# Row-grouped indexer scores, up-projected rotated halves, paired key norms and an exp/ln gate in a two-layer hybrid decoder

## What is computed

```python
for l in range(2):                        # x: (1, 512, 1024) float32
    x = x + token_mix(rms_norm(x), ...)   # three head groups, one input and one output projection
    x = x + square(relu(rms_norm(x) @ w_up)) @ w_down

# token_mix; proj = h @ w_in, split in columns
o_gla = rms_norm(gla(g_q, g_k, g_v, log_a)) * silu(g_gate)         # 4 heads x 128, chunks of 64
rel   = relu(einsum('bqhd,bsd->bqhs', iq, ik))                     # indexer: 8 heads of 32, one key
score = einsum('bqhs,bqh->bqs', rel, iw)                           # summed over heads, weighted
o_dsa = softmax attention over the 128 best causal keys of score   # 4 heads of 64
q_m   = heads(rms_norm(m_cq) @ mla_w_uq)                           # 192 -> 4 x 96 (64 + 32 rotary)
kv_m  = heads(rms_norm(m_ckv) @ mla_w_ukv)                         # 128 -> 4 x (64 key + 64 value)
q_m   = rms_norm(q_m); k_m = rms_norm(concat(k_nope, k_rope))      # over 96, per head
q_m, k_m: last 32 of 96 rotated: x1*cos - x2*sin, x2*cos + x1*sin  # k_rope shared by the heads
o_mla = causal softmax attention                                   # 4 heads, values of 64
out   = concat(o_gla, o_dsa, o_mla) @ w_out
```

## Time and profile before

| | |
|---|---|
| runs | 1363.98, 1358.61, 1358.93 us; median 1358.93 |
| the profiled execution | 1362.79 us, span 1361.1 us, mean granted clock 0.991 |
| TensorE matmul busy | 1305.0 us, 96% of the span, 5952 matmul records |
| VectorE, ScalarE, POOL busy | 812.4, 548.3, 252.3 us |
| DMA | 110.35 MB, 81 GB/s on average |

### The profile page before, as it was taken

One profiled execution on the slowest core, in us unless ns is written; L12 is line 12 of the kernel. 1 busy time (PEld: TensorE's weight loads), 2 busy tenths in 40 slices (PEclk: granted clock), 3 DMA queues, 4 the chain that ended last, 5 costly groups with the idle time before them and its releaser, 6 DMA issues.

```text
span 1361.1 us, 19335 instructions
## 1 busy us (share of the span) xinstructions
PE 1305.0 (96%) x5952; PEld 997.3 (73%) x5952; DVE 812.4 (60%) x1252; ACT 548.3 (40%) x875; POOL 252.3 (19%) x159
## 2 busy tenths in 40 slices
PE   4999999889999999999999999998999999999997
PEld 3755577568888888888885656874788888888886
DVE  4568887744454454544755888967345544445448
ACT  4465344744322313323434644357343232242334
POOL 5022231002011020110530322400020201102016
PEclk9999999989999999999999999999999999999999
DMA  5211121002332222322321111200132322232233
GB/s 199 94 32 63 47 78 47 1 16 95 114 104 97 93 92 95 105 92 92 107 81 62 63 47 62 94 1 1 47 117 98 102 92 93 92 103 97 92 102 129
DMA packets 31025, 110.35 MB, mean 81 GB/s; under 512 B 3568, under 2 KB 3568, under 8 KB 30832
## 3 DMA queue, kind: packets, MB, share of 16 engines
q1 hardware_dynamic: 29088, 103.82, 22.9%
q0 software_dynamic: 576, 3.63, 0.7%
q10 hardware_dynamic: 1296, 2.12, 0.5%
HBM read 107.46 MB, written 2.10 MB: 80 GB/s over the span
## 4 chain that ended last, share of the span: by engine, by line
PE 91%; DVE 3%; issue 2%; ACT 2%; POOL 1%; DMA 1%; DVEq 0%; ACTq 0%; SPq 0%; POOLq 0%
PE bank L816 17%; PE bank L815 17%; PE bank L817 17%; PE bank L477 6%; PE bank L479 6%; PE bank L478 6%; PE bank L511 2%; PE bank L603 2%; PE bank L499 2%; PE bank L500 2%; PE bank L498 2%; PE bank L704 1%; PE bank L731 1%; PE bank L716 1%; PE bank L688 1%
## 5 line engine op out<-in xcount | busy, mean ns | idle before, releaser
L870 ACT ACTIVATE wh<-raw 128x1024 fp32r<-128x1024 f32 x194 | 204.8, 1056 | 396.4 <-PE bank L817 239.0
L1132 DVE TENSOR_TENSOR wl<-raw,wh 128x1024 fp32r<-128x1024 f32 x158 | 247.0, 1563 | 96.1 <-ACT wh L870 88.5
L815 PE MATMUL bank<-hh,wl 128*128 128x512 f32 x512 | 200.0, 391 | 0.0
L815 PE MATMUL bank<-xmh,wl 128*128 128x512 f32 x512 | 199.3, 389 | 0.0
L817 PE MATMUL bank<-xml,wh 128*128 128x512 f32 x512 | 199.2, 389 | 0.0
L817 PE MATMUL bank<-hl,wh 128*128 128x512 f32 x512 | 199.2, 389 | 0.0
L816 PE MATMUL bank<-xmh,wh 128*128 128x512 f32 x512 | 199.2, 389 | 0.0
L816 PE MATMUL bank<-hh,wh 128*128 128x512 f32 x512 | 199.2, 389 | 0.0
L445 POOL TENSOR_TENSOR x<-x,rsb 128x512 f32<-128x512 f32 x64 | 86.7, 1355 | 578.2 <-DVE rsb L1496 578.2
L477 PE MATMUL bank<-xgh,wl 128*128 128x512 f32 x368 | 151.1, 411 | 24.0 <-DVE xgl L1141 18.4
L1485 DVE TENSOR_TENSOR sqb<-tf 128x512 f32<-128x512 f32 x64 | 44.3, 692 | 181.4 <-ACT hh L1103 181.4
(11 more groups left out here) (186 smaller groups left out, 1862.6 us busy)
## 6 DMA issues: line engine op xcount, KB each, us to landing
raw<-in_stream SPq DMA_DIRECT2D x194, 512.0 KB, 3.3
x<-in_x ACTq DMA_DIRECT2D x8, 256.0 KB, 12.8
out_y<-x SPq DMA_DIRECT2D x8, 256.0 KB, 4.1
par<-in_params POOLq DMA_DIRECT2D x2, 788.0 KB, 4.7
con<-in_consts POOLq DMA_DIRECT2D x1, 1200.5 KB, 9.7
par<-in_params POOLq DMA_DIRECT2D x1, 768.0 KB, 11.6
par<-in_params ACTq DMA_DIRECT2D x1, 20.0 KB, 2.5
```

The lines of the kernel that those rows point to most:

```text
L815: pe.matmul(B.t[s][:], wl[:, s, n_block(k)], src_h[:, k], start=(k == 0), stop=False)
L870: act.activation(wh[:, s], raw[:, s], ACT.Copy).then_inc(hi_ready.sem, 1)
L1132: vec.tensor_tensor(wl[:, s], raw[:, s], wh[:, s], ALU.subtract).then_inc(lo_ready.sem, 1)
```

## The change

Five edits are in the diff:
- **Relevance.** The index key is copied to the four groups of 32 partitions of one tile `ikr`. A head's matmul now contracts over its own 32 partitions of `iqT` and `ikr` only. `relevance(g)` waits for four vacant banks (2 to 5) and issues four heads. The six groups stand before, in the middle of, or behind units 7, 8 and 9. ScalarE's relus (`relevant(g)`) go to a new tile `rel` of three buffers, and both they and VectorE's additions (`weighted(g)`) are spread over slots 6, 7 and 8. The memset of `ikp` goes.
- **Rotated halves.** The up-projection's weights get 32 more columns per head, a copy of the rotary columns with swapped halves, so `mq` has 128 rows; `mrot` and its matmul go. The sign stands in the sine table, which lies on partitions 96 to 127 beside the cosine. The bank is now freed by VectorE's `mla_turn`.
- **Key norms by pairs.** The up-projection weights are laid out with keys and values apart, two heads' keys to a matmul; one statistic per pair, with the block matrix `blk`. ScalarE's `key_factor` writes the first head's factor a second time for the rotary rows.
- **Gate.** sigmoid(x) as exp(min(x, 0) - ln(1 + exp(-|x|))).
- **Order.** `mla_v` moves up by two units, the selection steps begin in slot 9 and end in slot 21. ScalarE waits for `gg_ready` before its first exponentials of attention.

```diff
+W_UK = W_UQ + 2 * H * P
+W_UV = W_UK + H * NOPE
...
-    + [(f"rel{i}", 2 + i % 2) for i in range(3 * IDX_H)]
+    + [(f"rel{i}", 2 + i % 4) for i in range(3 * IDX_H)]
...
-                pool.memset(ikp[:], 0.0).then_inc(zeroed.sem, 1)
...
-                for i, (qb, h) in enumerate(REL):
-                    pe.wait_ge(*B.vacant(l, f"rel{i}"))
-                    n = (qb + 1) * P
-                    pe.matmul(B[f"rel{i}"][:, 0:n], iqT[:, h // 4, qb * P:(qb + 1) * P], ikp[:, h % 4, 0:n],
-                              start=True, stop=True).then_inc(*B.on_fill(f"rel{i}"))
-                unit(7)
+                def relevance(g):
+                    for i in range(4 * g, 4 * g + 4):
+                        pe.wait_ge(*B.vacant(l, f"rel{i}"))
+                    for i in range(4 * g, 4 * g + 4):
+                        qb, h = REL[i]
+                        n = (qb + 1) * P
+                        r = slice(32 * (h % 4), 32 * (h % 4) + 32)
+                        pe.matmul(B[f"rel{i}"][:, 0:n], iqT[r, h // 4, qb * P:(qb + 1) * P], ikr[r, 0:n],
+                                  start=True, stop=True).then_inc(*B.on_fill(f"rel{i}"))
+                def midway(g):
+                    return lambda k: relevance(g) if k == KB // 2 else None
+                relevance(0)
+                unit(7, before=midway(1))
...
-                unit(8)
+                relevance(2)
+                unit(8, before=midway(3))
...
-                unit(9)
+                relevance(4)
+                unit(9, before=midway(5))
...
-                def mla_q_rest(h):
+                def mla_q_stat(h):
                     stat(l, f"mqst{h}", ones[0:QK, 0:QK], sq_of(f"mqst{h}")[0:QK], QK)
-                    pe.wait_ge(*qg_ready.at(l, h))
-                    pe.wait_ge(*B.vacant(l, f"mrot{h}"))
-                    pe.matmul(B[f"mrot{h}"][64:QK], con[64:QK, C_ROT:C_ROT + ROPE], tf[64:QK, h % 2],
-                              start=True, stop=True).then_inc(*B.on_fill(f"mrot{h}"))
...
+                def mla_k(pr):
+                    c = W_UK + pr * 2 * NOPE
+                    pe.matmul(B[name][:], par[:, c:c + 2 * NOPE], ckvn[:], start=True, stop=True)\
...
+                def mla_k_stat(pr):
+                    pe.matmul(B[name][:], blk, sq_of(name), start=True, stop=False)
+                    pe.matmul(B[name][:], ones[64:QK, :], cqn[64:QK, 1], start=False, stop=True)\
...
+                def relevant(g):
+                    for i in range(4 * g, 4 * g + 4):
+                        act.wait_ge(*B.filled(l, f"rel{i}"))
+                        if i >= 3:
+                            act.wait_ge(*rel_used.at(l, i - 3))
+                        act.activation(rel[:, i % 3, 0:n], B[f"rel{i}"][:, 0:n], ACT.Relu)\
...
+                def mla_turn(h):
+                    vec.wait_ge(*q_copied.at(l, h))
+                    vec.tensor_tensor(tf[64:QK, h % 2], tf[64:QK, h % 2], cos, ALU.mult)
+                    vec.scalar_tensor_tensor(qT[64:QK, h], B[f"mq{h}"][QK:P, :], gain(G_MQ, QK, P), sin,
+                                             ALU.mult, ALU.mult).then_inc(*B.on_read(f"mq{h}"))
...
+                        link(act.activation(gate_of(h), gg[:, h], ACT.Abs))
+                        link(act.activation(gate_of(h), gate_of(h), ACT.Exp, scale=-1.0))
+                        act.activation(gate_of(h), gate_of(h), ACT.Ln, bias=ones[:, 0:1]).then_inc(gexp_ready.sem, 1)
...
-                per_slot = {7: 5, 8: 4, 9: 4, 10: 3, 11: 3, 12: 4, 13: 4, 14: 4, 15: 4, 16: 2, 17: 2, 18: 2,
-                            19: 2, 20: 5}
+                per_slot = {9: 4, 10: 4, 11: 4, 12: 4, 13: 4, 14: 4, 15: 4, 16: 4, 17: 3, 18: 3,
+                            19: 3, 20: 4, 21: 3}
```

More of the change, by code:

```diff
@@ L194 @@
 NORMS = (["cqst", "ckvst", "dqst0", "mqst0", "dqst1", "mqst1", "dkst0", "mqst2", "dkst1", "mqst3"]
-         + [f"mkst{h}" for h in range(H)] + [f"gst{h}" for h in range(GLA_H)]
+         + ["mkst0", "mkst1"] + [f"gst{h}" for h in range(GLA_H)]
          + [f"aost{b}" for b in range(4)])
@@ L246, in build_trunk @@
         iqT, a0 = place("iqT", [P, 2, T])
-        ikp, _ = place("ikp", [P, 4, T])
+        ikr, _ = place("ikr", [P, T])
+        rel, _ = place("rel", [P, 3, T])
         st, _ = place("st", [P, NCHUNK, 2, GLA_DV], at=a0)
@@ L560, in mla_k_stat @@
                     pe.wait_ge(*B.vacant(l, name))
-                    pe.matmul(B[name][0:QK], ones[0:NOPE, 0:QK], sq_of(name)[0:NOPE], start=True, stop=False)
-                    pe.matmul(B[name][0:QK], ones[64:QK, 0:QK], cqn[64:QK, 1], start=False, stop=True)\
+                    pe.matmul(B[name][:], blk, sq_of(name), start=True, stop=False)
+                    pe.matmul(B[name][:], ones[64:QK, :], cqn[64:QK, 1], start=False, stop=True)\
                         .then_inc(*B.on_fill(name))
@@ L637, in _ @@
                 alone(pe)
-                pe.matmul(B["krot"][64:QK], con[64:QK, C_ROT:C_ROT + ROPE], kT[64:QK, 2],
-                          start=True, stop=True).then_inc(*B.on_fill("krot"))
+                pe.matmul(B["krot"][QK:P], con[64:QK, C_ROT:C_ROT + ROPE], kT[64:QK, 2],
+                          start=True, stop=True, tile_position=(64, QK)).then_inc(*B.on_fill("krot"))
                 mla_k(0)
@@ L944, in tasks @@
                         act.activation(glrs[:], B["glr"][0:RANK, :], ACT.Copy).then_inc(*B.on_read("glr"))
-                        for i, (qb, h) in enumerate(REL):
-                            n = (qb + 1) * P
-                            act.wait_ge(*B.filled(l, f"rel{i}"))
-                            if i >= 2:
-                                act.wait_ge(*rel_used.at(l, i - 2))
-                            act.activation(sqb[:, i % 2, 0:n], B[f"rel{i}"][:, 0:n], ACT.Relu)\
-                                .then_inc(*B.on_read(f"rel{i}"))
+                        relevant(0)
+                        relevant(1)
                     if u == 7:
@@ L996, in tasks @@
                         factor("mqst3", QK, QK)
-                        square("mkst0", B["mk0"][0:NOPE, :], slice(0, NOPE), wait=B.filled(l, "mk0"))
-                    if 14 <= u <= 17:
-                        if u < 17:
-                            h = u - 13
-                            square(f"mkst{h}", B[f"mk{h}"][0:NOPE, :], slice(0, NOPE), wait=B.filled(l, f"mk{h}"))
-                        factor(f"mkst{u - 14}", QK, QK)
-                    if u in (17, 18):
-                        i = u - 17
+                        square("mkst0", B["mk0"][:], wait=B.filled(l, "mk0"))
+                    if u == 14:
+                        square("mkst1", B["mk1"][:], wait=B.filled(l, "mk1"))
+                    if u in (14, 15):
+                        key_factor(u - 14)
+                    if u in (15, 16):
+                        i = u - 15
                         act.wait_ge(*B.filled(l, f"mv{i}"))
@@ new lines, in log_gate, with weighted @@
+                def log_gate(h):
+                    vec.wait_ge(*gexp_ready.at(l, h))
+                    vec.scalar_tensor_tensor(gate_of(h), gg[:, h], 0.0, gate_of(h), ALU.min, ALU.subtract)\
+                        .then_inc(gmin_ready.sem, 1)
+                def silu(h):
+                    vec.wait_ge(*sig_ready.at(l, h))
+                    vec.tensor_tensor(gg[:, h], gg[:, h], gate_of(h), ALU.mult).then_inc(gg_ready.sem, 1)
+                def weighted(g):
+                    for i in range(4 * g, 4 * g + 4):
+                        qb, h = REL[i]
+                        n = (qb + 1) * P
+                        dst = scores_of(qb)
+                        vec.wait_ge(*B.freed(l, f"rel{i}"))
+                        after(vec.scalar_tensor_tensor(dst, rel[:, i % 3, 0:n], iws[:, qb - 1, h:h + 1],
+                                                       causal(qb) if h == 0 else dst, ALU.mult, ALU.add),
+                              rel_used.sem, rel_used.at(l, i)[1])
@@ L1270, in tasks @@
                         evacuate("cq", cqn[:, 0])
-                        for i, (qb, h) in enumerate(REL):
-                            n = (qb + 1) * P
-                            dst = scores_of(qb)
-                            vec.wait_ge(*B.freed(l, f"rel{i}"))
-                            after(vec.scalar_tensor_tensor(dst, sqb[:, i % 2, 0:n], iws[:, qb - 1, h:h + 1],
-                                                           causal(qb) if h == 0 else dst, ALU.mult, ALU.add),
-                                  rel_used.sem, rel_used.at(l, i)[1])
+                        weighted(0)
+                        weighted(1)
                     if u == 7:
@@ L1614, in constant_block @@
         c[64 + half * r:64 + half * (r + 1), C_COS:C_COS + T] = np.cos(ang)
[L1615 removed]
+        c[QK + half * r:QK + half * (r + 1), C_COS:C_COS + T] = np.sin(ang) * (2 * r - 1)
     return c
```

169 lines of the change are left out of this document (93 added, 76 removed), and 15 rows, old and new, of the table USES.

## The result

| | before | after |
|---|---|---|
| median of 7 runs each, measured side by side | 1359.22 us | 1343.55 us |
| lowest to highest | 1358.61 to 1364.52 | 1340.75 to 1352.68 |
| the profiled execution, its span, its mean clock | 1362.79, 1361.1, 0.991 | 1343.55, 1341.9, 0.983 |

The ratio is 0.9874, with an interval from 0.9853 to 0.9896: faster by 1.3%, 15.7 us between the medians, 19.2 between the two profiled spans. The prediction was 34.6 us and a range from 1308 to 1341. The sign was right, the size less than half, and the time outside the range.

A forecast was written before the change was run, and what follows sets the result against it. It took TensorE as the bound, busy 1305.0 of 1361.1 us, so only its work or waits count. 2 x (9.3 behind unit 9 + 8.0 in relevance) = 34.6 us off the median 1358.9 gave 1324.3 us, range 1308 to 1341.

The forecast's parts named there:

- items 1 and 2: Behind unit 9: dropping four rotation matmuls gains 3.9 us per layer, key norms by pairs 6.1.
- I take 0.7: At the second value bank: TensorE waits 0.7 us per layer for VectorE to free the second key pair's bank.
- the blocking of VectorE by POOL: Rival in units 7 to 9: relevance additions held by POOL's low parts, up to 11 us per layer slower, 1381; chance 0.03.
- zero by itself: The gate by exp and ln, behind unit 9: no gain of its own, as TensorE waits for none of it.
- Item 4, row groups: Relevance, units 7 to 9: four heads side by side take 1.06 us with 512 columns; six groups 5.1 us.
- Item 4, waits: Relevance, units 7 to 9: four TensorE waits of 0.9, 1.35, 3.2 and 1.65 us, 7.1 per layer.
- Gain 8.0: Relevance to unit 9's end: 33.6 us where it was 41.6, so 8.0 us per layer gained.
- TensorE's clock falls: Rival: the 3.2 us wait lowers the clock, some 1.7 us each, up to four times, 1331; within the forecast's 0.59.
- VectorE becomes the bound: Rival behind unit 9: VectorE keeps its idle times, items 1 to 3 give nothing, 1342.9 us; chance 0.12.
- Items 1 to 3: Behind unit 9: rotated halves, key norms by pairs and the gate together give 9.3 us per layer.
- One by one: Rival in relevance: matmuls of a group run in a row, gaining 2.9 us per layer there, 1334.5; chance 0.10.
- Attention itself changed in length: Sign of a wrong prediction: attention, taken as unchanged and given no gain, differs in length.

The follow-up runs named there:

- Experiment 3: The changed kernel with POOL's low part of each weight unit cut into four instructions of 128x256: 1332.15 us, ratio 0.9780.
- experiment 2: The changed kernel with six of the 48 selection steps moved from slots 12 to 15 to later slots: 1330.25 us, ratio 0.9771.
- Experiment 4: The changed kernel with the old gate (exponential, plus one, VectorE's reciprocal and product): 1355.4 us, ratio 0.9954.
- Experiment 6: The changed kernel with every relevance matmul on partitions 0 to 31, in the same order and places: 1363.94 us, ratio 1.0004.
- experiment 5: The changed kernel with all six relevance groups behind unit 6, all relus and additions in slot 6: 1360.48 us, ratio 0.9995.
- experiment 7: The changed kernel with ScalarE's two squares of the query latent moved between the first two groups of relus: 1344.62 us, ratio 0.9884.
- experiment 9: The changed kernel with later selection steps, earlier squares of the query latent and four relu buffers for three: 1320.32 us, ratio 0.9689.
- experiment 10: The changed kernel with later selection steps and four relu buffers, the squares left in place: 1319.34 us, ratio 0.9685.
- experiment 11: The changed kernel with later selection steps, earlier squares, four relu buffers and POOL's low parts in four pieces: 1316.06 us, ratio 0.9655.
- experiment 12: The kernel of experiment 9 with the second value bank computed three times over: 1317.93 us, ratio 0.9683.

## Why the prediction was wrong, point by point

**The account.** Forecast 34.6 us, measured 19.2 between the profiles, so 15.4 are missing. The two places of half clock cost 11.9, attention lost 3.4 less than before, so 8.5 are half clock and 6.9 the rest; 5.1 of these lie in the two stretches. In layer 1, with what the half clock cost taken out (3.4 and 2.8 us): the first is 32.5 (forecast 33.6), the second 107.2 (forecast 103.5). The second can be checked by its parts: 112.8 - 11.3 for items 1 and 2 + 5.6 of wait = 107.1.

- **Items 1 and 2, rotations and key norms: right.** Forecast 10.0 us per layer; with TensorE busy throughout, the stretch is 101.5 where it was 112.8, so 11.3. Of the 1.3 more, 0.8 are rotations: what stands between two units fell from 4.86 to 3.72 us in three places and from 3.78 to 2.48 in the fourth, 1.14 and 1.30 for a rotation priced at 0.97. The rest lies with the keys.
- **Item 3, "I take 0.7": this step failed.** It measured 5.6 us in each layer, and 2.8 and 2.3 us of half clock behind it. The layout had VectorE behind in slots 12 to 15, at the right place, with the right bank as the victim. It priced each instruction by its free duration. The prediction had the blocking of VectorE by POOL among its rivals, but asked it of the relevance additions alone ("one low part held up one addition"). It did not go through the slots of its own layout for instructions that read two tiles of SBUF and come beside a low part. There were eight per layer, where there had been two. The gate's new instruction, "about 0.7", measured 2.2 on average. Experiment 3 shows the cause; in experiment 2 the load fitted, once most of the holds had gone. The prediction had named the sign of this step failing: TensorE waiting for `kT` by more than 3 us per layer.
- **Item 3, "zero by itself": wrong in this kernel.** Experiment 4 puts the new gate at 11 to 12 us: with the old one, VectorE comes late to attention (5.1 us of waits on `gvt`). At 90% full, as the prediction had the stretch, the cover had no room for four reciprocals of 3.34.
- **Item 4, row groups: right.** 1.07 and 0.86 us for groups with 512 and 384 columns, forecast 1.06 and 0.85 from the pair of the earlier trace rows. By the Trainium skill's 3.07 ("TensorE: Matmul & The Clock Gate", section "Measured speedup vs the span model") it would be 1.12, an estimate. The "0.5 us a layer less good" that the prediction made of it is a slip: with its own prices the six groups come to 2 x (1.12 + 0.83 + 0.56) = 5.0 us, as its 5.1. The two changes of tiling mode don't show in a group; the unit's next matmul starts a step late (58.97 - 58.63 = 0.34 where a step is 0.23), so 0.11 per group in place of 0.32.
- **Item 4, waits: near, 4.7 us per layer for 7.1.** Measured 0.52 (0.9 forecast), 1.43 (1.35), 2.73 (3.2) and none (1.65). Missing was what the third does to the clock: 3.4 us. "Gain 8.0" measured 5.8.
- **The rival "TensorE's clock falls"** named the wait of 3.2 us, and 1.7 us each, up to four times. There were four stretches, of 3.4 us of lost clock each: two behind that wait, two at the value bank, partly within its wait. Its price came from one stretch of 4 us with clock 0.64, though the same trace has one of 6.8 us at half clock, from 950 to 957 (0.53, 0.50 and 0.50 in three stretches of 2 us, 0.77 in the next). At 11.9 us it would have been 1336 against the median, still inside the range: the half clock alone did not take the time out of it, the wait on `kT` came on top.
- **"VectorE becomes the bound", 1342.9,** has the measured time to within 1 us, which is luck, as the sum behind it is another. Items 1 to 3 did not give nothing: they gave 2.8 of 9.3 us per layer, and the groups less than their 8.0. It was right that slots 12 to 15 are the weak place, but VectorE lagged there by its holds, and not because it kept its idle times.
- **"One by one"** was given 1334.5. Experiment 6 shows what it costs: 1363.9, 20 us above the changed kernel where the prediction had 10, since such a group is followed by half clock as well.
- **"Attention itself changed in length"** stood among what would make the prediction wrong; it did, by the clock alone, and this time in its favour.

## What to carry to other kernels

When a change fills VectorE where it was cover, go through its new order beside GpSimd's, and price each instruction that reads two tiles of SBUF and falls beside one of GpSimd as lasting until that one has ended; move such instructions apart, or cut GpSimd's into pieces. Count a wait of TensorE with the half clock behind it: here a wait of 2.7 us cost 6.1, and taking 5 us of waits out gave 11. Judge a spread and a speed-up of a matmul together with its reader: faster row groups in one block gained nothing, since the copies and additions kept TensorE waiting and the clock fell.

## What the runs showed of the hardware

- The half clock shows in stretches of 3.4, 6.8 or 10.2 us in nearly all these traces (17 and 20 us in experiment 5). One wait of 2.73 us was followed by 6.8, one of 2.68 by none and one of 2.66 by 3.4 (experiment 7).
- TensorE without a gap also lost its clock, between 60 and 61 us, in the first group that stood on 32 rows of the array alone (experiment 6). Four groups of rows side by side did not do that.
- The clock differs between runs of one kernel: experiment 9 had 1315.67 us at 0.991 and 1324.34 at 0.984, experiment 6 from 1358.68 at 0.982 to 1373.97 at 0.970. Most of the spread of these medians is this, so differences of 3 us between experiments 9, 10, 11 and 12 mean nothing.
- Four instructions of 128x256 on POOL took 2.8 to 3.5 us (once 4.0) where one of 128x1024 took 2.4. VectorE gained nearly as much as POOL paid.
